# The opening of a hybrid decoder layer: zero products first, smaller first transfers, own rows and banks for the first pair, GpSimd for one product

## The chip, the core and the metric

The kernel runs on one core of one Trainium2 chip. The metric is the time of one execution in device microseconds (us). The median of three runs of the kernel before is 911.94 us (911.87 to 914.20). The data are float32; matrix products are made from high and low parts in a rounded float32 form.

## What is computed

One layer of a decoder with 512 tokens and 1024 features. Cut to what matters here:

```python
h = rmsnorm(x, g_mix)
q_sb, k_sb, v_sb, q_r, k_r, v_r, g_r, gate_sb, gate_ret = split_cols(h @ w_in)
q_sb = head_rmsnorm(to_heads(q_sb, 8), sb_q_gain)        # heads of 64
k_sb = head_rmsnorm(to_heads(k_sb, 8), sb_k_gain)
y_sb = from_heads(stick_breaking_attention(q_sb, k_sb, to_heads(v_sb, 8)))
q_r = rotary(to_heads(q_r, 8))
k_r = rotary(to_heads(k_r, 8)) * 64 ** -0.5
y_r = retention_chunkwise(q_r, k_r, to_heads(v_r, 8))
y_r = from_heads(head_rmsnorm(y_r, ret_norm_gain)) * silu(g_r)
merged = sigmoid(gate_sb) * (y_sb @ w_branch_sb) + sigmoid(gate_ret) * (y_r @ w_branch_ret)
x = x + merged @ w_out
# then a gated feed-forward block (w_up, a causal convolution, w_down) and a gated embedding
```

rmsnorm divides x by the root of its mean square over the 1024 features and multiplies by a gain per feature.

## The kernel before, in words

Features lie on partitions, so x is eight tiles of 128x512. A weight matrix is cut into chunks of 128 output columns; a chunk is eight blocks of 128x128 (512 KB) and its product with x or h is one PSUM bank. SP loads a chunk into one of three ring slots w_f, ScalarE casts it to w_hi (L644), VectorE makes w_lo = w_f - w_hi (L1068), and TensorE makes three products a block (split3, L346 to L348: high by high, high by low, low by high), 24 a chunk. The input tiles have a high and a low part in the same way.

The mixer goes by four pairs of heads. A pair takes nine chunks ("slots"), numbered 0 to 8 for the first pair: q, k, v of the attention, q and k of the retention, two of its gate, two of its v. Chunks 9 on belong to the second pair. Each engine has a program of its own, written out by hand; semaphores join them. TensorE's other work (statistics, transposes, scores, values) is hung between the blocks of chunks: a hook at place (s, k) runs behind block k of slot s (back, L495).

The first pair differs from the others, so that TensorE can begin before the norm is known. Chunks 0 to 7 are multiplied with x * g_mix (tiles T_X0), and the eviction evac_x (L1129) multiplies by A_RS = 1/rms(x), which stands in for the norm. Chunk 8 and everything later use h itself (tiles T_H), made beside chunks 2 to 8: normed (x * gain * A_RS), high_h (L812), low_h (L1125). Only chunk 8 waits for h's tiles one by one.

The opening, by engine:
- SP (L235 to L250): chunk 0, x in four transfers of two tiles, chunk 1, the constants, chunk 2, the rotary table, the decay rows; then chunks 3 to 7, each once its slot is free. Later swap_halves (L257) copies the halves of the rotary q and k.
- ScalarE: g_mix is loaded, the table loaded, w_hi of chunk 0 is cast; then x's eight tiles are cast with their gain (raw high parts), with two squares between; w_hi of chunk 1; the other six squares; w_hi of chunk 2; Ln and Exp of the mean square (A_RS).
- VectorE: w_lo of chunk 0, raw_split of the eight tiles (L1080), the sum of the squares (raw_sum, L1086), w_lo of chunks 1 and 2, six small constants, and then start() (L1286) and first_back() (L1313).
- TensorE: chunks 0, 1 and 2, with stat_x (the sum over partitions, L522) in chunk 1 and stat_qk (L366) for q's heads behind chunk 2.
- GpSimd issues seven small loads and does nothing else.

The dense banks are three (bank[s % 3]); free_bank (L476) makes slot s wait until slot s-3 is evicted. aty has three more banks: 0 for statistics and transposes, 0 and 1 for the turned weights, 2 for the values' sum. The attention of a pair is a chain over three groups of blocks: sb_scores (TensorE), sb_factors (ScalarE), sb_weights (VectorE scans), sb_turn (TensorE), sb_high and sb_low, sb_values. The values of the first head end in y_out (L749), which copies them from aty's bank 2 before the second head's values may write there. On ScalarE y_out stands behind high_rot(0, 0), the cast of the rotated q.

## Time and profile before

| | |
|---|---|
| median of three runs | 911.94 us |
| the profiled execution's own time | 913.93 us |
| its span, first to last instruction | 912.1 us |
| TensorE, work in flight | 892.4 us |
| VectorE busy | 517.4 us |
| ScalarE busy | 398.9 us |
| mean granted clock of TensorE | 0.998 of full |

The span is what the trace shows; 1.8 us of the execution lie around it. All times below are in us from the span's start. Products on TensorE overlap, so a product's length says little: their pitch, the distance between starts, is the cost. A row of the timeline gives the start, the length (of all that it merges), the engine, the line, the operation, output and inputs, the shape, how many, and, where the engine stood idle before it, for how long and what ended that.

### The profile page before, as it was taken

The page shows a single profiled execution, that of the slowest core. Times are in us where ns is not written, and L with a number is a line of the kernel's source. Part 1 is how long each engine was busy: PE and PEld are TensorE (multiplying, and loading weights), DVE is VectorE, ACT ScalarE, POOL GpSimd, SP SyncE. Part 2 cuts the span into 40 slices and gives each one's busy share as a digit, 9 for nine tenths or more (in the row PEclk, how much of TensorE's full clock was granted, in tenths as well). Part 3 has the DMA queues.
Part 4 walks back from the last instruction along what each step waited for, and adds up shares of the span by engine and source line. Part 5 has one row for each costly group of instructions (what it writes and reads, how often), then busy time and mean ns, then how long its engine had stood idle before and what let it go on. Part 6 is the DMA issues. An engine that isn't in the chain of part 4 may idle for free.

```text
span 912.1 us, 11455 instructions
## 1 busy us (share of the span) xinstructions
PE 892.4 (98%) x4070; PEld 724.4 (79%) x4070; DVE 517.4 (57%) x660; ACT 398.9 (44%) x519; POOL 4.0 (0%) x11
## 2 busy tenths in 40 slices
PE   6998999999999999999999999999999999999998
PEld 5776787787787888888887888888888888888786
DVE  6787577577677453333555666566655643333354
ACT  6636657557566442233244433333333332223431
POOL 1000000000000000000000000000000000000000
PEclk9999999999999999999999999999999999999999
DMA  7214214214213153322322332222222232322141
GB/s 275 80 36 139 81 36 138 80 35 138 80 35 127 58 196 104 104 82 91 115 94 96 115 111 92 92 92 92 100 107 92 86 104 87 103 86 93 58 143 70
DMA packets 28553, 89.93 MB, mean 99 GB/s; under 512 B 3920, under 2 KB 4960, under 8 KB 28400
## 3 DMA queue, kind: packets, MB, share of 16 engines
q1 hardware_dynamic: 27232, 85.87, 27.4%
q10 hardware_dynamic: 1072, 3.67, 1.2%
q8 instruction: 15, 0.25, 0.1%
q0 software_dynamic: 224, 0.06, 0.1%
q14 instruction: 10, 0.08, 0.0%
HBM read 84.34 MB, written 2.10 MB: 95 GB/s over the span
## 4 chain that ended last, share of the span: by engine, by line
PE 92%; DVE 4%; ACT 2%; issue 1%; DMA 1%; SPq 0%; ACTq 0%; DVEq 0%
PE dense L346 29%; PE dense L348 28%; PE dense L347 28%; PE z L402 2%; DVE fs L1068 1%; DVE w_lo L1068 1%; PE aty L431 1%; DVE fs L1071 1%; PE aty L446 1%; PE aty L391 1%; ACT fs L629 1%; ACT w_hi L644 1%; DMA fs<-in_xT 1%; PE aty L348 1%; PE aty L347 1%
## 5 line engine op out<-in xcount | busy, mean ns | idle before, releaser
L346 PE MATMUL dense<-hi,w_hi 128*128 128x512 f32 x1184 | 471.3, 398 | 9.3 <-DVE lo L1071 8.9
L348 PE MATMUL dense<-hi,w_lo 128*128 128x512 f32 x1184 | 462.7, 391 | 0.0
L347 PE MATMUL dense<-lo,w_hi 128*128 128x512 f32 x1184 | 462.6, 391 | 0.0
L1068 DVE TENSOR_TENSOR w_lo<-w_f,w_hi 128x1024 fp32r<-128x1024 f32 (+2 forms) x160 | 184.3, 1152 | 229.4 <-ACT w_hi L644 228.9
L346 PEld LDWEIGHTS dense<-hi,w_hi 128*128 128x128 f32 x1184 | 223.3, 189 | 60.4 <-issue 13.3
L348 PEld LDWEIGHTS dense<-hi,w_lo 128*128 128x128 f32 x1184 | 223.1, 188 | 47.4
L347 PEld LDWEIGHTS dense<-lo,w_hi 128*128 128x128 f32 x1184 | 223.5, 189 | 44.4 <-issue 1.2
L644 ACT CAST w_hi<-w_f 128x1024 fp32r<-128x1024 f32 (+2 forms) x160 | 158.3, 990 | 181.3 <-PE dense L348 179.0
L629 ACT ACTIVATE fs<-fs 128x512 f32<-128x512 f32 (+2 forms) x79 | 55.3, 707 | 80.7 <-DVE fs L1068 41.5
L1068 DVE TENSOR_TENSOR fs<-fs 128x512 f32<-128x512 f32 (+2 forms) x119 | 87.7, 742 | 3.9 <-ACT fs L676 0.5
L1068 DVE TENSOR_TENSOR lo<-fs,hi 128x512 fp32r<-128x512 f32 (+3 forms) x73 | 54.5, 755 | 40.9 <-ACT hi L1003 20.1
L1068 DVE TENSOR_TENSOR fs<-dense,fs 128x512 f32<-128x512 f32 x84 | 57.4, 684 | 8.4 <-ACT fs L629 5.0
L1071 DVE SCALAR_TENSOR_TENSOR fs<-fs,cw 128x512 f32<-128x512 f32 x44 | 33.1, 751 | 28.0 <-ACT fs L629 25.0
L1003 ACT CAST hi<-fs 128x512 f32 (+1 forms) x22 | 13.7, 621 | 59.5 <-DVE fs L1068 59.5
L629 ACT ACTIVATE fs<-fs,cw 128x512 f32<-128x512 f32 x22 | 17.9, 816 | 43.8 <-DVE fs L1068 43.8
L1071 DVE SCALAR_TENSOR_TENSOR lo<-fs,gain,hi 128x512 fp32r<-128x512 f32 (+1 forms) x24 | 17.7, 750 | 24.3 <-ACT hi L629 24.3
L1071 DVE SCALAR_TENSOR_TENSOR fs<-fs,gain 128x512 f32<-128x512 f32 x24 | 17.5, 748 | 20.6 <-ACT fs L629 20.6
L1244 DVE TENSOR_TENSOR_SCAN fs<-z,mrev 128x511 f32<-128x511 f32 (+3 forms) x32 | 24.1, 804 | 3.9 <-ACT z L629 3.8
L783 ACT CAST hi<-aty 128x512 fp32r<-128x512 f32 (+1 forms) x16 | 10.7, 696 | 32.4 <-PE aty L431 32.4
L727 ACT CAST hi<-z 128x1024 fp32r<-128x1024 f32 (+3 forms) x16 | 11.1, 695 | 30.9 <-DVE z L1068 30.9
L629 ACT ACTIVATE fs<-aty,eps 128x512 f32<-128x512 f32 (+1 forms) x15 | 12.0, 803 | 19.6 <-PE aty L383 8.1
L1068 DVE TENSOR_TENSOR lo<-z,hi 128x1024 fp32r<-128x1024 f32 (+3 forms) x16 | 13.2, 825 | 12.2 <-ACT hi L727 12.2
(87 smaller groups left out, 379.8 us busy)
## 6 DMA issues: line engine op xcount, KB each, us to landing
w_f<-in_w_in SPq DMA_DIRECT2D x52, 512.0 KB, 3.3
w_f<-in_w_up SPq DMA_DIRECT2D x44, 512.0 KB, 3.1
w_f<-in_w_down SPq DMA_DIRECT2D x16, 512.0 KB, 3.5
w_f<-in_w_b SPq DMA_DIRECT2D x8, 512.0 KB, 3.2
w_f<-in_w_out SPq DMA_DIRECT2D x8, 512.0 KB, 3.2
w_f<-in_w_pg SPq DMA_DIRECT2D x8, 512.0 KB, 3.2
w_f<-in_w_down SPq DMA_DIRECT2D x8, 384.0 KB, 3.0
fs<-in_xT SPq DMA_DIRECT2D x4, 512.0 KB, 7.0
```

Of the source, the lines that this page charges most:

```text
L346: mm(out, w1, x1, start=start, stop=False, skip_group_check=skip)
L347: mm(out, w1, x0, start=False, stop=False, skip_group_check=skip)
L348: return mm(out, w0, x1, start=False, stop=stop, skip_group_check=skip)
L402: ins = mm(z[:, hd, first_col:first_col + cols.stop - cols.start], wp[rows, w, i * P:(i + 1) * P], xp[rows, x, cols], start=first, stop=last)
L629: return nc.scalar.activation(out, src, func, **kw).then_inc(done, 1)
L644: nc.scalar.copy(w_hi[r][:, 0:kt, :], w_f[r][:, 0:kt, :]).then_inc(s_whi, 1)
L727: nc.scalar.copy(r_pair(hi, i), z[:, :, 0:width(i)]).then_inc(s_rahi, 1)
L783: ins = nc.scalar.copy(at_blocks(hi)[:, :, to, :], aty[:, 0:2, first:first + n].rearrange("p h (b c) -> p h b c", c=P))
L1003: nc.scalar.copy(hi[:, T_G + f, :], fs[:, A_U, :]).then_inc(s_ghi, 1)
L1068: return nc.vector.tensor_tensor(out, a, b, op).then_inc(done, 1)
L1071: return nc.vector.scalar_tensor_tensor(out=out, in0=a, scalar=scalar, in1=b, op0=op0, op1=op1).then_inc(done, 1)
L1244: nc.vector.tensor_tensor_scan(fs[:, A_CP + hd, to + skip:to + width], z[:, hd, last - skip:last - width:-1], mrev[:, skip:width], 0.0, AL ...
```

## The change

It touches only the opening and the first pair.
- Zeros: VectorE writes zeros into a tile, and TensorE makes ten products of 128x512 with it into aty's bank 2 before chunk 0.
- Loads: chunk 0 in two halves of 256 KB; x as one tile on SP, one, two and two tiles on ScalarE's queue, and two on SP. The casts and w_lo of chunk 0 are in halves too, the second ahead of x's tile 2.
- The constants made by VectorE (ones, block, mask, reversed identity) are made by GpSimd.
- stat_x moves to block 2 of chunk 2. On VectorE w_lo of chunk 2 goes ahead of the last two sums, and w_lo of chunk 3 ahead of the wait for A_RS.
- The first pair's q and k go to rows A_G and A_G+1 and no longer wait for h's first tiles, and both are evicted and squared one right behind the other.
- Slots 3 and 4 of the first pair go to aty's banks 1 and 2, so only slots 5 and 8 wait for evictions.
- x * A_RS is made by GpSimd, in place, eight products behind one another; the gain moves into high_h and low_h.
- Hooks of the first pair move: scores 1 from (5, 2) to (5, 0), scores 2 from (6, 3) to (6, 1), values and turns by one place or more.
- The order on ScalarE and VectorE in start and first_back changes with it.

```diff
-            load(0, 0, w_in[0], 8, first=True)
-            for i in range(4):
-                load_x(i)
+            sp.dma_start(w_f[0][:, 0:4, :], w_in[0][:, 0:4, :]).then_inc(s_w0, 16)
+            sp.dma_start(fs[:, A_X, :], xT[:, 0, :]).then_inc(s_x[0], 16)
+            sp.dma_start(w_f[0][:, 4:8, :], w_in[0][:, 4:8, :]).then_inc(s_wdma[0], 16)
+            sp.dma_start(fs[:, A_X + 4:A_X + 6, :], xT[:, 4:6, :]).then_inc(s_x[3], 16)
...
+            pool.wait_ge(s_xrs, 1)
+            for n in H_ORDER:
+                x = fs[:, A_X + n, :]
+                nc.gpsimd.tensor_tensor(x, x, fs[:, A_RS, :], ALU.mult).then_inc(s_hf, 1)
...
                 if g == 0:
                     pe.wait_ge(s_raw_done, RAWS * j + 3)
-                    if not isinstance(j, int):
+                    if isinstance(j, int):
+                        pe.wait_ge(s_evac, 4)
...
+            def warm_up():
+                pe.wait_ge(s_warm, 1)
+                for _ in range(10):
+                    mm(aty[:, 2, :], hi[:, T_SQ, 0:P], hi[:, T_SQ, :], start=True, stop=True)
...
-                places = {(5, 2): at(sb_scores, j, 1), (5, 3): at(sb_turn, j, 0), (6, 0): at(sb_values, j, 0, 3),
-                          (6, 3): at(sb_scores, j, 2), (6, 4): at(sb_turn, j, 1), (7, 0): at(sb_values, j, 0, 2),
-                          (7, 2): at(sb_turn, j, 2), (7, 5): at(sb_values, j, 0, 1), (7, 6): at(sb_values, j, 0, 0),
-                          (8, 0): at(sb_values, j, 1, 3), (8, 1): at(sb_values, j, 1, 2),
-                          (8, 2): at(sb_values, j, 1, 1), (8, 3): at(sb_values, j, 1, 0),
+                    places = {(3, 1): at(stat_qk, 0, 1, (s_misc, 1)), (3, 7): at(sb_scores, j, 0),
+                              (4, 2): at(turn_v, 0, 2, (s_misc, 2)), (5, 0): at(sb_scores, j, 1),
+                              (5, 2): at(sb_turn, j, 0), (5, 7): at(sb_values, j, 0, 3), (6, 1): at(sb_scores, j, 2),
+                              (6, 3): at(sb_turn, j, 1), (7, 0): at(sb_values, j, 0, 2), (7, 3): at(sb_turn, j, 2),
+                              (7, 6): at(sb_values, j, 0, 1), (7, 7): at(sb_values, j, 0, 0)}
+                    later = 1
...
+                places[8, later] = at(sb_values, j, 1, 3)
+                places[8, later + 1] = at(sb_values, j, 1, 2)
...
                 for s in range(3, SLOTS):
-                    free_bank(j, s)
+                    if prev is not None or s in (5, 8):
+                        free_bank(j, s)
...
+                    out = aty[:, s - 2, :] if prev is None and s in (3, 4) else None
...
+            warm_up()
             chunk(0, 0, 0, KD, T_X0, before={k: (s_xlo, k + 1) for k in range(KD)})
-            chunk(1, 1, 1, KD, T_X0, {6: stat_x})
-            chunk(2, 2, 2, KD, T_X0, {7: lambda: stat_qk(0, 0, (s_xrs, 1))})
+            chunk(1, 1, 1, KD, T_X0)
+            chunk(2, 2, 2, KD, T_X0, {2: stat_x, 7: lambda: stat_qk(0, 0, (s_xrs, 1))})
...
             act.dma_start(gain[:, G_MIX:G_MIX + KD, 0], g_mix).then_inc(s_gmix, 16)
+            for i, n in ((1, 1), (2, 2), (4, 6)):
+                act.dma_start(fs[:, A_X + n:A_X + n + min(i, 2), :], xT[:, n:n + min(i, 2), :]).then_inc(s_x[i], 16)
...
+            act.wait_ge(s_w0, 16)
+            nc.scalar.copy(w_hi[0][:, 0:4, :], w_f[0][:, 0:4, :]).then_inc(s_w0hi, 1)
...
+                if k == 2:
+                    act.wait_ge(s_wdma[0], 16)
+                    nc.scalar.copy(w_hi[0][:, 4:8, :], w_f[0][:, 4:8, :]).then_inc(s_whi, 1)
```

ScalarE's start() and first_back(), before and after:

```diff
                 high(0, 2, first=True)
+                ahead(0, 1)
                 act.wait_ge(s_xst, 1)
                 run(fs[:, A_RS, :], misc, ACT.Ln, s_xln, scale=1.0 / D, bias=eps[:, :])
                 act.wait_ge(s_xln, 1)
                 run(fs[:, A_RS, :], fs[:, A_RS, :], ACT.Exp, s_xrs, scale=-0.5)
+                ahead(0, 2)
+                norm_qk(0, 0, 1)
                 high_h(0)
-                ahead(0, 1)
-                high_h(1)
-                norm_qk(0, 0, 1)
-                ahead(0, 2)
                 high_qk(0, 0)
                 norm_qk(0, 1, 2)
+                high_qk(0, 1)
                 sigmoid_tables()
-                high_qk(0, 1)
-                high_h(2)
-                high_h(4)
+                high_h(1)
+                ahead(0, 3)
```

VectorE's start():

```diff
+                ahead(0, 1)
                 dve.wait_ge(s_xrs, 1)
-                normed(0)
-                normed(1)
-                low_h(0)
+                dve.wait_ge(s_cr, 2)
+                dve.wait_ge(s_cp, 6)
                 evac_x(0)
                 square(0, 0)
-                ahead(0, 1)
-                low_h(1)
                 evac_x(1)
                 square(0, 1)
-                normed(2)
+                ahead(0, 2)
                 norm(0, 0)
-                ahead(0, 2)
+                low_h(0)
                 low_qk(0, 0)
                 norm(0, 1)
                 low_qk(0, 1)
-                low_h(2)
-                normed(4)
+                low_h(1)
                 evac_x(2)
+                ahead(0, 3)
```

In VectorE's first_back() the five normed go, evac_x(6) and low_h(6) move ahead of sb_low(0, 2), and low_h(3) and low_h(5) one group later.

## Rows read from the trace of the kernel before

**Rows 1.** The page's first part: busy us, share of the span, instructions.
```profile
PE 892.4 (98%) x4070; PEld 724.4 (79%) x4070; DVE 517.4 (57%) x660; ACT 398.9 (44%) x519; POOL 4.0 (0%) x11
```

**Rows 2.** Windows: stretch, length, busy (count) by engine, clock, DMA share, GB/s.
```profile
0.00:10.00 10.00, 1.79 (x4) 1.50 (x5) 3.92 (x6) 5.64 (x8) 4.03 (x11) 1.00 0.77 266
...
70.00:80.00 10.00, 8.15 (x33) 6.92 (x34) 7.12 (x11) 8.18 (x10) 0.00 (x0) 0.83 0.59 197
```

**Rows 3.** Waits of TensorE, 0 to 140 us: total, times, longest.
```profile
PE dense L346 <- DVE lo L1071: 8.2, 1, 8.2
PE aty L446 <- ACT fs L752: 2.5, 1, 2.5
PE aty L446 <- DVE lo L1264: 1.7, 2, 1.3
PE z L402 <- DVE lo L1068: 0.6, 1, 0.6
PE aty L431 <- DVE lo L1196: 0.5, 1, 0.5
```

**Rows 4.** The chain that ended last, 0 to 8 us: start, us, what.
```profile
1.19 5.27 DMA fs<-in_xT
...
6.48 0.73 ACT hi L629
```

**Rows 5.** Timeline of TensorE, 8 to 22 us.
```profile
8.21 0.77 PE L346 MATMUL dense<-hi,w_hi 128*128 128x512 f32 x1 [8.21 <-DVE lo L1071]
...
9.20 0.63 PE L348 MATMUL dense<-hi,w_lo 128*128 128x512 f32 x1
...
13.04 0.63 PE L348 MATMUL dense<-hi,w_lo 128*128 128x512 f32 x1
...
16.41 0.39 PE L346 MATMUL dense<-hi,w_hi 128*128 128x512 f32 x1
...
21.17 1.02 PE L364 MATMUL aty<-fs,cst 128*128 128x512 f32 x2
```

**Rows 6.** Timeline of ScalarE, 0 to 24 us.
```profile
0.75 0.42 ACTq L635 DMA_DIRECT2D gain<-in_g_mix  x1
...
4.62 1.04 ACT L644 CAST w_hi<-w_f 128x1024 fp32r<-128x1024 f32 x1 [2.13 <-DMA gain<-in_g_mix]
...
13.69 3.42 ACT L629 ACTIVATE fs<-fs 128x512 f32<-128x512 f32 x6
...
22.95 0.63 ACT L629 ACTIVATE fs<-fs 128x512 f32<-128x512 f32 x1
```

**Rows 7.** Timeline of VectorE, 5 to 27 us.
```profile
5.69 1.23 DVE L1068 TENSOR_TENSOR w_lo<-w_f,w_hi 128x1024 fp32r<-128x1024 f32 x1 [4.82 <-ACT w_hi L644]
7.32 2.88 DVE L1071 SCALAR_TENSOR_TENSOR lo<-fs,gain,hi 128x512 fp32r<-128x512 f32 x4 [0.40 <-ACT hi L629]
...
14.96 4.67 DVE L1068 TENSOR_TENSOR fs<-fs 128x512 f32<-128x512 f32 x6
...
26.66 0.69 DVE L1068 TENSOR_TENSOR fs<-fs 128x512 f32<-128x512 f32 x1
```

**Rows 8.** Timeline of TensorE: behind scores 0, first of chunk 8, first of chunk 9.
```profile
37.44 0.50 PE L346 MATMUL dense<-hi,w_hi 128*128 128x512 f32 x1
...
68.51 0.39 PE L346 MATMUL dense<-hi,w_hi 128*128 128x512 f32 x1
...
80.05 0.40 PE L346 MATMUL dense<-hi,w_hi 128*128 128x512 f32 x1
```

**Rows 9.** Timeline of VectorE: the first scans, the last residue of the rotary k.
```profile
43.18 2.33 DVE L1244 TENSOR_TENSOR_SCAN fs<-z,mrev 128x511 f32<-128x511 f32 x2
...
78.67 0.69 DVE L1068 TENSOR_TENSOR lo<-fs,hi 128x512 fp32r<-128x512 f32 x1 [0.69 <-ACT hi L706]
```

**Rows 10.** Timeline of ScalarE: y_out of the first head.
```profile
71.22 0.58 ACT L752 COPY fs<-aty 128x512 f32<-128x512 f32 x1
```

**Rows 11.** Timeline of GpSimd, 0 to 10 us: one of its four memsets.
```profile
0.25 0.10 POOL L1650 MEMSET const-float32-0.0<- 128x1 f32 x1 [0.25 <-issue]
```

More of the change, by code:

```diff
@@ L119, in build @@
         s_cst, s_gmix, s_gain, s_eps, s_cr = sem("s_cst"), sem("s_gmix"), sem("s_gain"), sem("s_eps"), sem("s_cr")
-        s_x = [sem(f"s_x{i}") for i in range(4)]
+        s_x = [sem(f"s_x{i}") for i in range(5)]
+        s_warm, s_w0, s_w0hi, s_cp = sem("s_warm"), sem("s_w0"), sem("s_w0hi"), sem("s_cp")
         s_xsq, s_xst, s_rope, s_dec = sem("s_xsq"), sem("s_xst"), sem("s_rope"), sem("s_dec")
@@ L167, in a_sq, with a_raw @@
             return A_T + t if isinstance(j, int) else A_SQ
+        def a_raw(j, t):
+            return A_G + t if isinstance(j, int) else A_RAW + t
         def keys(i):
@@ L348, in split3, with chunk @@
                 return mm(out, w0, x1, start=False, stop=stop, skip_group_check=skip)
-            def chunk(c, r, b, kt, tile0, hooks=None, k_first=0, last=True, before=None):
-                pe.wait_ge(s_wlo, c + 1)
+            def chunk(c, r, b, kt, tile0, hooks=None, k_first=0, last=True, before=None, out=None):
+                if not (isinstance(c, int) and c == 0):
+                    pe.wait_ge(s_wlo, c + 1)
+                out = bank[b][:, :] if out is None else out
                 for k in range(kt):
@@ L355, in chunk @@
                         pe.wait_ge(*before[k])
-                    ins = split3(bank[b][:, :], w_hi[r][:, k, :], w_lo[r][:, k, :], hi[:, tile0 + k, :],
+                    ins = split3(out, w_hi[r][:, k, :], w_lo[r][:, k, :], hi[:, tile0 + k, :],
                                  lo[:, tile0 + k, :], start=(k_first + k == 0), stop=(last and k == kt - 1))
@@ L514, in back @@
+                places[8, later] = at(sb_values, j, 1, 3)
+                places[8, later + 1] = at(sb_values, j, 1, 2)
+                places[8, later + 2] = at(sb_values, j, 1, 1)
+                places[8, later + 3] = at(sb_values, j, 1, 0)
+                places[8, 6] = at(turn_v, j, 7, (s_atlo, 3 * j + 3))
                 for s in range(3, SLOTS):
-                    free_bank(j, s)
+                    if prev is not None or s in (5, 8):
+                        free_bank(j, s)
                     hooks = {k: places[s, k] for k in range(KD) if (s, k) in places}
@@ L519, in back @@
                               for k in range(KD)} if prev is None and s == RAW_X else None
-                    chunk(SLOTS * j + s, s % RING, s % 3, KD, T_X0 if raw else T_H, hooks, before=before)
+                    out = aty[:, s - 2, :] if prev is None and s in (3, 4) else None
+                    chunk(SLOTS * j + s, s % RING, s % 3, KD, T_X0 if raw else T_H, hooks, before=before, out=out)
             def stat_x():
@@ L840, in first_back @@
                 sb_factors(0, 0)
-                ahead(0, 3)
                 high_v(0, 0)
-                high_h(3)
+                high_h(2)
                 ahead(0, 4)
-                high_h(5)
+                high_h(4)
                 sb_high(0, 0)
                 sb_factors(0, 1)
+                high_h(3)
                 ahead(0, 5)
+                high_h(5)
                 sb_high(0, 1)
                 sb_factors(0, 2)
+                ahead(0, 6)
                 high_h(6)
-                ahead(0, 6)
                 sb_high(0, 2)
@@ L1094, in raw_sum @@
                     tt(acc, acc, sq, ALU.add, s_xacc)
-            low(0, 0)
+            dve.wait_ge(s_w0hi, 1)
+            nc.vector.tensor_tensor(w_lo[0][:, 0:4, :], w_f[0][:, 0:4, :], w_hi[0][:, 0:4, :], ALU.subtract)
             dve.wait_ge(s_gmix, 16)
             for k in range(KD):
+                if k == 2:
+                    dve.wait_ge(s_whi, 1)
+                    tt(w_lo[0][:, 4:8, :], w_f[0][:, 4:8, :], w_hi[0][:, 4:8, :], ALU.subtract, s_wlo)
                 raw_split(k)
@@ L1313, in first_back @@
             def first_back():
-                low_h(4)
-                ahead(0, 3)
-                normed(3)
                 sb_weights(0, 0)
```

95 lines of the change are left out of this document (51 added, 44 removed).

## The prediction

> **What bounds the kernel now.** I read the page's busy times first. TensorE has work in flight for 98% of the span, VectorE for 57%, ScalarE for 44%, GpSimd for almost nothing [rows 1]. So one engine sets the end, and a change gains only where it takes time from TensorE: idle time, a lower clock, or work. The windows show where that time lies: in the first 10 us TensorE works 1.79 us, and in 70 to 80 us its granted clock is 0.83 [rows 2]. The waits up to 140 us then name it: 8.2 us before the first product, and 2.5, 1.7 (in two), 0.6 and 0.5 us later [rows 3]. After the first pair hardly anything is left, so this change has the first 80 us to work in.
>
> The opening is slower than its waits. From 9.20 to 13.04 nine products start 0.427 us apart, from 16.41 to 21.17 twenty-one start 0.227 us apart [rows 5]. These are the two levels of the clock, 1.2 and 2.4 GHz, though the column of the granted clock reads 1.00 in the first 10 us [rows 2]: the pitch is the surer sign. TensorE had idled for 8.2 us before the low stretch and for 2.5 us before the second one (71.85, clock 0.83). A chunk is 24 products: 24 * 0.227 = 5.45 us at full clock. I number the chunks of w_in 0 to 8; before, chunk 0 starts at 8.21, chunk 1 at 16.41, chunk 8 at 68.51 and chunk 9 at 80.05 [rows 5, 8].
>
> **The change part by part: the start.** Before, x's first pair of tiles lands at 6.46 (1.19 + 5.27), ScalarE's cast takes 0.73 us and VectorE's residue 0.76, and TensorE starts at 8.21 [rows 4, 5]. After, 256 KB of weights and 256 KB of x replace 512 and 512 KB on SP's queue, but ScalarE's queue moves x's other tiles at the same time. ScalarE's three added issues, 0.42 us each [rows 6], delay its table load by 1.3 us, which the wait to 4.62 covers. The first tile is bounded below by g_mix, which released ScalarE at 4.62 [rows 6], and above by today's 6.46. I take 5.0: cast to 5.7, residue to 6.5, TensorE at 6.6, 1.6 us earlier (bounds 0 to 2.0).
>
> From there VectorE paces chunk 0, not TensorE. It does eight residues at 0.72 us (2.88 for four), two sums (0.4 and 0.6), and now also the second half of w_lo, 0.6 us (half of 1.23) [rows 7]. That half waits for the second weight transfer and its cast; I put it at 7.4 to 8.1. Six residues and two sums later it is 13.3; w_lo of chunk 1 ends at 14.7. TensorE, at 0.68 us a tile, follows and starts chunk 1 at 14.8, where it was 16.41: 1.6 us. The full clock gains nothing beyond that, and TensorE could stay at the low level until near 11 us without being later. So the ten zero products (10 * 0.427 = 4.3 us, from 1.5 on, before any real work can start) cost nothing and are worth between 0 and 1.5 us.
>
> **Sum of x squared.** stat_x moves from chunk 1, tile 6, to chunk 2, tile 2. VectorE sums four squares (0.76 each), makes w_lo of chunk 2 (1.22, after ScalarE's cast that follows six squares of 0.57), sums two more and ends near 20.6 [rows 6, 7]. Chunk 2 starts at 20.3, stat_x is at 22.3, so TensorE doesn't wait. From stat_x to the end of Exp it is 2.4 us (21.17 to 22.95 + 0.63 [rows 5, 6]); 1/rms is there at 24.7, against 23.6. The six small constants move to GpSimd beside this; as they stood they took VectorE 1.4 us that nobody waited for.
>
> **q and k.** Before, VectorE does two products of x, two residues and two w_lo among the q and k steps; now q and k have rows A_G and A_G+1, and chunks 3 and 4 go to aty's banks 1 and 2, so TensorE needs no eviction before chunk 5. I walk it with single durations (0.69 for 512 columns and 1.22 for w_lo [rows 7], 0.63 for Exp and about the same for Ln [rows 6], and the 2.4 us again from a statistic to its Exp): eviction 25.4, square 26.1, stat_qk 26.6, Exp 29.0, norm 29.8, second Ln 30.4 to 31.7, norm 32.5, cast 33.1, residue 33.8. TensorE ends chunk 3 at 33.9, and its first scores no longer wait: their 0.6 us [rows 3] goes. Chunk 4 begins at 35.0, against 37.44 [rows 8]: 2.4 us ahead in all.
>
> **The middle.** The new places put scores 1 at (5,0), 2 at (6,1), and the values one or more tiles later. Two scans take 2.33 us [rows 9], so the first are done at 40.5, before (5,0) at 41.6; the turn at 44.1 finds v's residue (43.0) and the weights (41.7). values(0,3) comes at 48.5 against 47.4. Scores 2 come at 50.3, the scans end at 50.8: a new stall of 0.5. The next turn and values find their data. So the two stalls before today's values (1.7 together [rows 3]) and 0.5 of the first turn go, 0.5 comes, and shorter switches give 0.4: 2.1 us. Chunk 8 begins 4.5 us ahead, near 64.0.
>
> **Chunk 8** takes 11.5 us today. values(1,3) wait 2.5 us for ScalarE's copy y_out (71.22 [rows 10]), queued behind the cast of the rotated q, which waits for VectorE; then the clock is low: 0.83 over 10 us [rows 2] is 3.4 us at half speed, which costs 1.7. After, VectorE ends the first q's rotation at 64.2 (behind it no product of x any more), y_out ends at 65.4, and TensorE, now two tiles into the chunk, is at 65.3. The wait of 2.5 shrinks to 0.1 or so, the clock stays: with 0.2 for a switch, 3.9 us gained. Ahead by 8.4 us, chunk 9 starts near 71.6.
>
> **What is late next.** The second rotation doesn't move as much: VectorE still waits for chunk 7 and for the swap that SP starts after s_rot. low_rot(0,1), today at 78.67 to 79.36 [rows 9] with over 2 us in hand, would end at 73.0; r_scores ask at 73.0; then turn_v waits 0.45 for low_v(0,1), and r_scores 1 0.1. I book 0.8 back (bounds 0 to 2.5). SP's loads behind the swaps still land before their casts. Ahead: 7.6 us.
>
> **GpSimd.** It now makes eight products x * 1/rms of 128x512 from 24.7 on. No row shows such an operation on it: the nearest are a memset of one column, 0.10 us [rows 11], and VectorE's product of the same size, 0.69 [rows 7]. Alone it is hidden: the first is wanted by 29.0 (4.3 us), the second by 34.4 (9.7 us for two), later ones later still. ScalarE waits for them, and behind that high_h(1) stand w_hi of chunk 5 and the factors of the scores. But GpSimd works beside VectorE for the first time, in the stretch where VectorE's chain leads. There VectorE has ten operations, 7.6 us, in 9.1 us, so 1.5 us of slack, and eight of them read two tensors from SBUF. If each waits w, the delay is 8w - 1.5. With w = 0 it is nothing, with w a whole product of 0.69 it is 4.0 us. I take half a product, 1.3 us. (The Trainium skill, "SBUF — State Buffer", section "Who interferes with whom", says that a VectorE instruction with two SBUF inputs contends with a GpSimd instruction that reads SBUF. "GPSIMD Engine Reference", section "3. Performance versus the Vector engine", gives GpSimd 1.96 times VectorE's time for such an operation, by which a product would be 1.35 us, an estimate, and with whole products waited for the delay 9.3 us. No run here shows either yet.)
>
> **Sum.** 1.6 (start) + 0 (pace, same 1.6 at chunk 1) + 0.8 (scores) + 2.1 + 3.9 = 8.4; less 0.8 and 1.3: 6.3 us. Profiled, 913.93 - 6.3 = 907.6 with a span of 905.8. That execution is 2.0 above the median of 911.94, and the forecast stands against the median: 905.6 us.
>
> **Rivals.**
> 1. The wait that replaces the removed ones: VectorE and GpSimd hold each other up by whole products, w from 0.69 to 1.35. Then the scores come 4.0 to 9.3 us late and the gain is 3.6 to -1.7: 908.3 to 913.6, middle 911. For it: the eight operations lie just in that stretch; against: VectorE has gaps of its own there, waiting for Ln and Exp. Chance 0.20. (The skill's rule in its strict form is this case.)
> 2. The transfers aren't sooner. Weights and x share the same total rate over two queues; x's first tile lands at 6.46 as today. VectorE's pace from there gives chunk 1 at 16.1, 1.3 us later than booked: 906.9, to 908 if the clock is low too. Chance 0.15.
> 3. It ends slower: the same mutual wait with w over 1.15 us takes all of the 7.6, and over 1.5 us makes the kernel more than 0.3% slower. At w = 1.7 the delay is 12.1 us: 916.4. It would need a GpSimd product over twice VectorE's. Chance 0.07.
> 4. No contention and nothing given back: 911.94 - 8.4 = 903.5, and to 902 if other steps come out better. Chance 0.08.
>
> My forecast, with a delay between 0 and 3 us, has the remaining 0.50. Over 0.3% (2.7 us, about what a measurement of this kernel can tell from no change) means below 909.2 or above 914.7. Faster: 0.50 + 0.15 + 0.08 and a fifth of rival 1, 0.77; within: 0.16; slower: 0.07. The range from 902.0 to 910.0 takes in all but the worse half of rival 1 and rival 3.
>
> **What would show it.** Right: first real product at 6.2 to 7.4; ten products before it at 0.43 us; chunk 1 at 14.8; no wait before the first scores; values(1,3) waiting under 0.7 us with the pitch at 0.227; chunk 9 near 73. Wrong: VectorE's squares, norms and residues between 24 and 36 us longer than 0.69, or starting late with their inputs ready; GpSimd products over 1.4 us; ScalarE waiting for GpSimd before high_h(1); or waits of TensorE over 1 us in the first chunks of pair 1.

## The result, and the profile after

The changed kernel takes 915.61 us, median of eleven runs (914.60 to 915.96). The kernel before, run beside it, takes 913.72 (eleven runs, 911.67 to 914.97). The ratio is 1.0025, with a 95% interval of 1.0015 to 1.0035. That is 0.25% slower, inside the 0.3% that the prediction called no change, and 10 us above its 905.6. The three runs shown before the prediction had a median of 911.94; 1.8 us of the 10 are that. The times of the kernel before fall into two groups, which the mean granted clock tells apart: of 29 later executions twelve read 1.00 and took 911.45 to 912.23 us, seventeen read 0.996 or 0.998 and took 913.21 to 915.31. The median of 911.94 lies in the first group, the profiled execution (913.93, clock 0.998, low in chunk 8 [rows 2]) in the second. None of the changed kernel's eleven runs reads 1.00 (0.992 to 0.998).

The profiled execution took 915.40 us with a span of 913.6. Comparing starts on TensorE in the traces splits the difference of the spans. The column e1 is the first experiment below (GpSimd's products cut to one column each); "forecast" is the prediction's own walk.

| us | before | after | e1 | forecast |
|---|---|---|---|---|
| start of chunk 1 | 16.41 | 16.90 | 17.21 | 14.8 |
| chunk 1 to scores 0 | 20.14 | 24.34 | 19.30 | 20.6 |
| scores 0 to chunk 8 | 31.96 | 32.06 | 29.53 | 29.9 |
| chunk 8 | 11.54 | 7.74 | 7.74 | 7.6 |
| chunk 9 to the end | 832.05 | 832.56 | 832.52 | 832.9 |
| span | 912.1 | 913.6 | 906.3 | 905.8 |

Three things stand in it: the opening isn't faster, chunk 8 gives what it should (3.8 of 3.9), and the stretch before the first scores has grown by 4.2 us.

The page's first part, to set beside [rows 1]: TensorE's work is what it was plus ten products, and GpSimd now has work.

```profile
PE 895.8 (98%) x4080; PEld 725.8 (79%) x4080; DVE 518.8 (57%) x649; ACT 400.2 (44%) x520; POOL 22.2 (2%) x25
```

VectorE has 11 instructions less and is busy 1.4 us more. Eight products of about 0.7 us (5.6 us), some small constants and more have left it, so what stayed must have become longer. That is visible before any timeline is opened.

The waits of TensorE from 0 to 140 us, where [rows 3] stood before (total, times, longest):

```profile
PE z L419 <- DVE lo L1109: 5.1, 2, 4.9
PE dense L361 <- DVE lo L1112: 3.8, 4, 1.5
PE aty L501 <- DVE hi L1121: 1.5, 1, 1.5
...
PE aty L467 <- ACT fs L792: 0.2, 1, 0.2
```

The 8.2 us wait at the start has been cut into 1.5 before the zeros and 3.8 before and in chunk 0, the wait for y_out has gone from 2.5 to 0.2, and the 1.7 before the first values is gone. On top stands a new one: 4.9 us before the first scores, for a residue of VectorE. It was 0.6.

The windows (stretch, length, busy and count of TensorE, its weight loads, VectorE, ScalarE and GpSimd, then clock, DMA share, GB/s), as in [rows 2]:

```profile
30.00:40.00 10.00, 6.38 (x27) 4.58 (x25) 9.51 (x6) 4.23 (x7) 10.00 (x6) 1.00 0.14 54
...
40.00:50.00 10.00, 8.76 (x31) 6.57 (x32) 8.34 (x11) 7.57 (x11) 0.63 (x1) 0.66 0.15 52
```

From 30 to 40 us VectorE is busy 9.51 us with six instructions, 1.6 us each, while GpSimd has no gap. From 40 to 50 the clock is at 0.66.

TensorE's timeline gives the starts of the table and the price of the low clock, against [rows 5, 8]:

```profile
1.49 4.57 PE L501 MATMUL aty<-hi 128*128 128x512 f32 x10 [1.49 <-DVE hi L1121]
...
7.44 0.50 PE L361 MATMUL dense<-hi,w_hi 128*128 128x512 f32 x1 [1.37 <-DVE lo L1112]
...
16.90 0.50 PE L361 MATMUL dense<-hi,w_hi 128*128 128x512 f32 x1 [0.44 <-DVE w_lo L1109]
...
41.24 0.80 PE L419 MATMUL z<-hi 64*128 64x512 f32 x2 [4.86 <-DVE lo L1109]
...
43.41 0.63 PE L362 MATMUL aty<-lo,w_hi 128*128 128x512 f32 x1
...
45.97 0.63 PE L362 MATMUL aty<-lo,w_hi 128*128 128x512 f32 x1
...
73.30 0.39 PE L361 MATMUL dense<-hi,w_hi 128*128 128x512 f32 x1
```

From 43.41 to 45.97 lie six products, 0.427 us each: after idling for 4.86 us TensorE is at 1.2 GHz, half of its full speed, until 46.8 us. In the kernel before it idled 0.6 us here and stayed at the full level.

### The profile page after: what moved, and what is told of

It is laid out like the page before. It is cut to its first block, busy times and chain, and to the rows that moved or that the text cites. A ratio compares the mean times of both kernels' runs of the same rounds, so it can differ in the third digit from the quotient of the medians.

```text
span 913.6 us, 11479 instructions
## 1 busy us (share of the span) xinstructions
PE 895.8 (98%) x4080; PEld 725.8 (79%) x4080; DVE 518.8 (57%) x649; ACT 400.2 (44%) x520; POOL 22.2 (2%) x25
## 4 chain that ended last, share of the span: by engine, by line
PE 92%; DVE 4%; ACT 2%; DMA 1%; issue 0%; SPq 0%; ACTq 0%; DVEq 0%
PE dense L361 28%; PE dense L363 28%; PE dense L362 28%; PE z L419 2%; DVE fs L1109 1%; DMA fs<-in_xT 1%; PE aty L450 1%; DVE w_lo L1109 1%; PE aty L361 1%; PE aty L363 1%; PE aty L362 1%; DVE lo L1112 1%; PE aty L408 1%; PE aty L467 0%; DVE fs L1112 0%
## 5 line engine op out<-in xcount | busy, mean ns | idle before, releaser
L361 PE MATMUL dense<-hi,w_hi 128*128 128x512 f32 x1168 | 462.8, 396 | 5.3 <-DVE lo L1112 4.5
L363 PE MATMUL dense<-hi,w_lo 128*128 128x512 f32 x1168 | 455.1, 390 | 0.0
L362 PE MATMUL dense<-lo,w_hi 128*128 128x512 f32 x1168 | 455.0, 390 | 0.0
L361 PEld LDWEIGHTS dense<-hi,w_hi 128*128 128x128 f32 x1168 | 219.3, 188 | 57.3 <-DVE lo L1112 7.4
L363 PEld LDWEIGHTS dense<-hi,w_lo 128*128 128x128 f32 x1168 | 219.2, 188 | 46.4
L362 PEld LDWEIGHTS dense<-lo,w_hi 128*128 128x128 f32 x1168 | 219.5, 188 | 43.1 <-issue 0.7
L1109 DVE TENSOR_TENSOR lo<-fs,hi 128x512 f32 (+3 forms) x65 | 50.5, 785 | 40.2 <-ACT hi L1044 20.1
L1112 DVE SCALAR_TENSOR_TENSOR lo<-fs,gain,hi 128x512 fp32r<-128x512 f32 (+1 forms) x32 | 24.7, 783 | 26.8 <-ACT hi L664 25.8
L1112 DVE SCALAR_TENSOR_TENSOR fs<-fs,gain 128x512 f32<-128x512 f32 x16 | 13.7, 877 | 18.9 <-ACT fs L664 18.9
L1308 DVE TENSOR_TENSOR lo<-aty,hi 128x512 fp32r<-128x512 f32 (+1 forms) x16 | 12.8, 822 | 14.6 <-ACT hi L823 14.6
```

The lines of the kernel that those rows point to most:

```text
L361: mm(out, w1, x1, start=start, stop=False, skip_group_check=skip)
L362: mm(out, w1, x0, start=False, stop=False, skip_group_check=skip)
L363: return mm(out, w0, x1, start=False, stop=stop, skip_group_check=skip)
L1109: return nc.vector.tensor_tensor(out, a, b, op).then_inc(done, 1)
L1112: return nc.vector.scalar_tensor_tensor(out=out, in0=a, scalar=scalar, in1=b, op0=op0, op1=op1).then_inc(done, 1)
L1308: ins = nc.vector.tensor_tensor(at_blocks(lo)[:, :, to, :], aty[:, 0:2, first:first + n].rearrange("p h (b c) -> p h b c", c=P), at_blocks ...
```

## The cause on VectorE

GpSimd's eight products are one row of its timeline, and VectorE's work beside them ten:

```profile
27.01 13.62 POOL L352 TENSOR_TENSOR fs<-fs 128x512 f32<-128x512 f32 x8 [8.98 <-ACT fs L664]
```

```profile
26.96 0.69 DVE L1109 TENSOR_TENSOR fs<-dense,fs 128x512 f32<-128x512 f32 x1 [2.78 <-ACT fs L664]
27.69 1.17 DVE L1109 TENSOR_TENSOR fs<-fs 128x512 f32<-128x512 f32 x1
28.78 0.68 DVE L1109 TENSOR_TENSOR fs<-dense,fs 128x512 f32<-128x512 f32 x1
29.49 1.04 DVE L1109 TENSOR_TENSOR fs<-fs 128x512 f32<-128x512 f32 x1
30.46 2.31 DVE L1109 TENSOR_TENSOR w_lo<-w_f,w_hi 128x1024 fp32r<-128x1024 f32 x1
32.70 1.78 DVE L1112 SCALAR_TENSOR_TENSOR fs<-fs,gain 128x512 f32<-128x512 f32 x1
34.40 1.77 DVE L1112 SCALAR_TENSOR_TENSOR lo<-fs,gain,hi 128x512 fp32r<-128x512 f32 x1
36.10 1.75 DVE L1109 TENSOR_TENSOR lo<-fs,hi 128x512 fp32r<-128x512 f32 x1
37.77 1.75 DVE L1112 SCALAR_TENSOR_TENSOR fs<-fs,gain 128x512 f32<-128x512 f32 x1
40.20 0.99 DVE L1109 TENSOR_TENSOR lo<-fs,hi 128x512 fp32r<-128x512 f32 x1 [0.69 <-ACT hi L742]
```

The two evictions (fs<-dense,fs) read one tensor from PSUM and one from SBUF: 0.69 and 0.68, as before [rows 7]. All the others read twice from SBUF: 0.99 to 1.78 in place of about 0.7, 2.31 in place of 1.22. The least stretched are the two squares, which read one tensor twice (1.17 and 1.04), and the last, beside which GpSimd ends. Nothing starts late; the operations themselves are longer. These are the eight that the prediction named. From 32.70 on the two engines go in step: VectorE starts an operation at 32.70, 34.40, 36.10 and 37.77, and GpSimd makes its eight in 13.62 us, 1.70 each. Whether one stands still while the other reads, or both read at a lower rate, these rows can't tell.

## The experiments

Each is the changed kernel with one edit, unless said otherwise. The kernel before ran beside every group; the medians of those runs lie between 913.4 and 913.8, and each ratio is taken against them.

**e1: take GpSimd's products away, keep their order and waits.** Only one column of each x tile is multiplied by 1/rms.

```diff
-                nc.gpsimd.tensor_tensor(x, x, fs[:, A_RS, :], ALU.mult).then_inc(s_hf, 1)
+                nc.gpsimd.tensor_tensor(x[:, 0:1], x[:, 0:1], fs[:, A_RS, 0:1], ALU.mult).then_inc(s_hf, 1)
```

> The changed kernel with GpSimd's eight products of x made on one column instead of 512 (the rest of h isn't scaled: work left out). Theory, contention: VectorE's squares, norms and residues between 27 and 41 us take 0.69 to 0.75 us again instead of 1.0 to 1.8, low_qk(0,1) ends near 35.5, the scores' wait falls from 4.9 to under 0.5 us, the clock doesn't fall, so 4.7 + 2.3 = 7 us less: about 908.7 us. Rival, order: the operations put ahead of the norms (w_lo of chunk 4, low_h(0)) make the scores late; then the wait stays above 3 us and the time near 914. Rival, late 1/rms: the same, because stat_x came at 24.5.

Measured: 908.21 us, ratio 0.9950 (0.9935 to 0.9965). VectorE's same operations, from its timeline:

```profile
28.04 0.72 DVE L1109 TENSOR_TENSOR fs<-fs 128x512 f32<-128x512 f32 x1
...
30.00 1.22 DVE L1109 TENSOR_TENSOR w_lo<-w_f,w_hi 128x1024 fp32r<-128x1024 f32 x1
31.62 0.76 DVE L1112 SCALAR_TENSOR_TENSOR fs<-fs,gain 128x512 f32<-128x512 f32 x1 [0.40 <-ACT fs L664]
...
33.06 0.69 DVE L1109 TENSOR_TENSOR lo<-fs,hi 128x512 fp32r<-128x512 f32 x1
```

The stretch is gone, operation by operation; over the eight it had been 6.3 us (0.45 + 0.35 + 1.09 + 1.02 + 1.02 + 1.06 + 0.99 + 0.30). The scores start at 36.51 in place of 41.24. The price of the products is 915.61 - 908.21 = 7.4 us: 4.7 of later scores (5.0 counted from chunk 1), and 2.5 in the stretch behind them (32.06 against 29.53), where the clock now reads 1.00 in 40 to 50 us. These 2.5 lie where the clock was low: from the first scores to the next transposes it is 5.59 us in the change (41.24 to 46.83) and 3.06 here (36.51 to 39.57), for the same products.

**e6: the products back on VectorE, in its gaps.** Eight instructions normed(k), where the changed order waits for ScalarE anyway.

```diff
-            for n in H_ORDER:
-                x = fs[:, A_X + n, :]
-                nc.gpsimd.tensor_tensor(x, x, fs[:, A_RS, :], ALU.mult).then_inc(s_hf, 1)
...
+                normed(0)
                 norm(0, 0)
                 low_h(0)
                 low_qk(0, 0)
+                normed(1)
                 norm(0, 1)
+                normed(2)
                 low_qk(0, 1)
+                normed(4)
+                normed(3)
                 low_h(1)
```

> The changed kernel with x times 1/rms back on VectorE (eight products of 0.69 us, put in VectorE's gaps), nothing else undone. Theory: VectorE has 4.8 us more to do but none of its operations is stretched, so the scores wait under 1 us and the time is within 1.5 us above the 908.2 of the kernel with one-column products: 908.5 to 909.7, faster than both. Rival, VectorE's load: the eight products cost 0.6 us each on the chain and the time is 912 to 913.

Measured: 909.02 us, ratio 0.9952 (0.9936 to 0.9968); scores at 37.11. (One of its six executions took 3563.4 us, and one of the kernel before beside it 2303.9; neither is in the ratio, and without it the median is 908.89.) With all the work done, it costs 0.8 us more than e1, with none of it done (within the runs' scatter), and 6.6 us less than GpSimd doing it. VectorE has gaps for its eight products of about 0.65 us; as GpSimd's neighbour it loses 6.3 us.

**e8: is it any work of GpSimd, or two tensors read at once?** The product becomes one by a constant 1.0, with one tensor read (1/rms is left out).

```diff
-                nc.gpsimd.tensor_tensor(x, x, fs[:, A_RS, :], ALU.mult).then_inc(s_hf, 1)
+                nc.gpsimd.tensor_scalar(x, x, 1.0, None, ALU.mult).then_inc(s_hf, 1)
```

> The changed kernel with GpSimd's eight products by a tensor replaced by products by the constant 1.0 (one input instead of two; x isn't scaled: work left out). If what holds VectorE up is each access of GpSimd to SBUF, VectorE's two-input operations between 27 and 41 us are still stretched, but by about half (1.0 to 1.3 us), and the scores wait 1.5 to 3 us: 911 to 913. If only a second input of GpSimd's collides, they take 0.7 us and the time is near 908.5.

Measured: 908.88 us, ratio 0.9952 (0.9934 to 0.9970). GpSimd is as busy as ever, and VectorE hardly notices:

```profile
27.48 12.97 POOL L352 TENSOR_SCALAR fs<-fs 128x512 f32<-128x512 f32 x8 [9.32 <-ACT fs L664]
```

```profile
30.09 1.22 DVE L1109 TENSOR_TENSOR w_lo<-w_f,w_hi 128x1024 fp32r<-128x1024 f32 x1
...
33.17 0.99 DVE L1109 TENSOR_TENSOR lo<-fs,hi 128x512 fp32r<-128x512 f32 x1
34.43 1.19 DVE L1112 SCALAR_TENSOR_TENSOR fs<-fs,gain 128x512 f32<-128x512 f32 x1 [0.26 <-ACT fs L664]
```

GpSimd's eight, by their source line (shortest, median and longest in ns):

```profile
L352 POOL TENSOR_SCALAR fs<-fs x8: 1482/1496/2249, 27.5 to 38.8; 128x512 f32<-128x512 f32 x8
```

w_lo keeps its 1.22 us, and the worst operation is 1.19 in place of 0.76. The eight lose 0.8 us together (0.30, 0.43 and 0.08 on three of them) where they had lost 6.3. So with one tensor read GpSimd still collides with VectorE, but little of it falls on VectorE: it is GpSimd's product beside w_lo that takes 2.25 us, where its median is 1.50. Nearly all of the price hangs on GpSimd's second tensor, or on the kind of operation, which changed with it; no run separates these two. e8 also clears GpSimd's slowness as such: its results come nearly as late as with the real products (the last at 40.45 against 40.63), and nothing waits for them long enough to matter.

**e11: the kernel before, with only the products moved to GpSimd.** High_h and low_h take the gain, as in the change; nothing else is touched.

```diff
+            pool.wait_ge(s_xrs, 1)
+            for n in H_ORDER:
+                x = fs[:, A_X + n, :]
+                nc.gpsimd.tensor_tensor(x, x, fs[:, A_RS, :], ALU.mult).then_inc(s_hf, 1)
...
-                nc.scalar.copy(hi[:, T_H + k, :], fs[:, A_X + k, :]).then_inc(s_hhi, 1)
+                nc.scalar.activation(hi[:, T_H + k, :], fs[:, A_X + k, :], ACT.Identity,
+                                     scale=gain[:, G_MIX + k, :]).then_inc(s_hhi, 1)
```

> The kernel before with one part of the change alone: x times 1/rms on GpSimd, the gain in the high and low parts of h. Theory, contention: VectorE's two-input operations from 24 to 38 us are stretched from 0.69 to 1.0 to 1.8 us, which costs more than the four products of 0.75 us that leave VectorE there; the scores come 3 to 6 us later than 36.55, the clock falls in the wait, and the time is 4 to 8 us longer than the kernel before: 917 to 922 us. Rival, it was the new order that made it costly: the time is within 2 us of before.

Measured: 912.76 us, ratio 0.9993 (0.9983 to 1.0003): a miss for me. The stretch is there (w_lo at 2.28 us) and the scores are 4.6 us late (41.16 against 36.55), as expected, but the end is not. Its waits behind the start's show why (1.5 is that for y_out, 2.5 before):

```profile
PE aty L368 <- DVE fs L1073: 1.8, 2, 1.6
PE aty L450 <- ACT fs L756: 1.5, 1, 1.5
PE z L406 <- DVE lo L1073: 1.3, 1, 1.3
PE dense L350 <- DVE w_lo L1073: 1.2, 1, 1.2
```

```profile
28.90 2.28 DVE L1073 TENSOR_TENSOR w_lo<-w_f,w_hi 128x1024 fp32r<-128x1024 f32 x1
```

The delay is taken in pieces of 1.2 to 1.6 us, since chunks wait for evictions between, and no window from 30 to 80 us has a clock under 1.00. Behind the scores it gets back 3.0 us up to chunk 8 (28.97 against 31.96) and 2.5 in chunk 8 (9.03 against 11.54), where VectorE and the clock were what TensorE waited for before. The changed kernel has hardly any such waits left: with everything else of the change in place, moving the products only lost. The same edit makes next to no difference in one order of work and costs 6.6 us in the other (915.61 against e6's 909.02). Next to none, since e11's twelve runs all read a clock of 1.00 or 0.999: it is 1.0 us slower than the runs of the kernel before that read 1.00 (median 911.73 in this group), and 1.4 faster than the median of the others, 914.14. That the removed waits decide is read from these two traces; no run puts them back into the changed kernel.

**e3: the first transfers and casts of the kernel before, in the changed kernel.**

```diff
+            load(0, 0, w_in[0], 8, first=True)
+            for i in range(4):
+                sp.dma_start(fs[:, A_X + 2 * i:A_X + 2 * i + 2, :], xT[:, 2 * i:2 * i + 2, :]).then_inc(s_x[i], 16)
...
-            for i, n in ((1, 1), (2, 2), (4, 6)):
-                act.dma_start(fs[:, A_X + n:A_X + n + min(i, 2), :], xT[:, n:n + min(i, 2), :]).then_inc(s_x[i], 16)
```

> The changed kernel with the first transfers, casts and the residue of chunk 0 as before the change; zero products, order and GpSimd stay. Theory: TensorE starts at 8.2 with the full clock, VectorE's pace ends chunk 1's w_lo at 15.1, chunk 1 starts near 15.2 against 16.9, so 1.7 us less: 913.9 us; the new transfers alone would then cost 1.7 us. Rival: the new transfers do help (first product 0.8 us sooner) and this kernel is 0.8 us slower, 916.4.

Measured: 914.03 us (914.45 profiled), ratio 1.0007 (0.9997 to 1.0017): 1.6 us faster than the change. The first product starts later, at 8.63 against 7.44, and chunk 1 sooner, at 16.09 against 16.90. The two kernels' runs don't overlap (913.08 to 914.58 against 914.60 to 915.96). So the early start of TensorE bought nothing.

**e2: the small transfers, all on SP's queue in the order of need.**

```diff
             sp.dma_start(fs[:, A_X, :], xT[:, 0, :]).then_inc(s_x[0], 16)
+            sp.dma_start(fs[:, A_X + 1, :], xT[:, 1, :]).then_inc(s_x[1], 16)
             sp.dma_start(w_f[0][:, 4:8, :], w_in[0][:, 4:8, :]).then_inc(s_wdma[0], 16)
-            sp.dma_start(fs[:, A_X + 4:A_X + 6, :], xT[:, 4:6, :]).then_inc(s_x[3], 16)
+            for i in (2, 3, 4):
+                n = 2 * i - 2
+                sp.dma_start(fs[:, A_X + n:A_X + n + 2, :], xT[:, n:n + 2, :]).then_inc(s_x[i], 16)
```

> The changed kernel with all first transfers on SP's queue in the order in which they are used: half of chunk 0, x tile 0, tile 1, other half, then x's pairs. Theory, order of arrival: the second half of chunk 0's weights lands near 6.5 instead of 8.4, chunk 1 starts near 15.0 instead of 16.9, and stat_x, the scores and the end come 1.8 us earlier: 913.8 us. Rival, total rate: the two queues share one rate and the same bytes must land either way, so chunk 1 starts within 0.4 us of 16.9.

Measured: 914.96 us, ratio 1.0021 (1.0011 to 1.0032), chunk 1 at 16.74, where 15.0 was expected; it stayed within the rival's 0.4 us of 16.90. The order over the two queues is worth some 0.65 us, less than what the opening lacks, and the interval overlaps the change's.

**e5: GpSimd's seven small loads after x.**

```diff
+            pool.wait_ge(s_x[4], 16)
             for col, src, n in
```

> The changed kernel with GpSimd's seven small loads (gains and convolution weights, 0.06 MB) issued only once x's last pair has landed. Theory, small packets: from 3 to 6 us the DMA engines are 0.83 to 1.03 busy but move only 156 to 253 GB/s, because the small packets of the gains take turns with the weights' and x's; without them the second half of chunk 0's weights lands near 7 instead of 8.4, chunk 1 starts near 15.4 instead of 16.9, and the time is 1.5 us less than the changed kernel's 915.6: 914.1. Rival, smaller transfers are slow by themselves: the landings stay within 0.4 us and the time too.

Measured: 914.72 us, ratio 1.0016 (1.0005 to 1.0027), chunk 1 at 16.53; 0.9 us faster than the change, with overlapping intervals, and not all of it is the loads'. In the profiled executions, 1.3 us apart, chunk 1 comes 0.4 sooner; 1.0 lies behind the scores, where after the same wait (4.85 us) the clock of 40 to 50 us reads 0.83 in place of 0.66. The windows of 3 to 6 us, first of the change, then of this kernel:

```profile
3.00:4.00 1.00, 1.00 (x4) 0.81 (x3) 0.00 (x0) 0.99 (x2) 1.00 (x3) 1.00 1.03 253
4.00:5.00 1.00, 1.00 (x3) 0.78 (x3) 0.43 (x1) 0.54 (x1) 1.00 (x3) 1.00 0.83 205
5.00:6.00 1.00, 1.00 (x3) 0.33 (x1) 0.27 (x1) 0.20 (x1) 0.65 (x2) 1.00 0.94 156
```

```profile
3.00:4.00 1.00, 1.00 (x4) 0.81 (x3) 0.00 (x0) 0.99 (x2) 0.00 (x0) 1.00 0.88 199
4.00:5.00 1.00, 1.00 (x3) 0.78 (x3) 0.41 (x1) 0.56 (x1) 0.00 (x0) 1.00 0.93 266
5.00:6.00 1.00, 1.00 (x3) 0.33 (x1) 0.28 (x1) 0.44 (x1) 0.00 (x0) 1.00 0.95 336
```

The last number is GB/s, the one before it the busy share of the DMA engines. With the small loads in flight the engines are as busy in these 3 us (2.80 against 2.76) and move 614 KB in place of 801. Over all traces with the change's new transfers or e2's it is 544 to 614 KB with the loads early (the change, e1, e2, e4, e6, e8) and 711 to 801 with them late (e5, e7, e10): the sign holds, the size varies. With the old transfers it doesn't show: 721 to 901 early (the kernel before, e3, e11), 806 and 818 late (e12, e9).

**e7: e6 and e5 together.**

> Both: x times 1/rms on VectorE, and GpSimd's small loads after x's last pair. If the two gains add, the time is 1.5 us below the one with the products on VectorE alone, near 907.5; if chunk 1's start doesn't move, they are the same.

Measured: 907.95 us, ratio 0.9945 (0.9929 to 0.9960); chunk 1 at 16.18, scores at 35.55. The late loads are worth 1.1 us here, with the clock at 1.00 behind the scores in both; e6's chunk 1 came at 17.73.

**e9: e7 with the first transfers of the kernel before.**

> The changed kernel with x times 1/rms on VectorE, GpSimd's small loads late, and the first transfers as before the change (512 KB each, all on SP). If larger transfers move x and the weights sooner, as they seemed to with the small loads early (1.6 us), chunk 1 starts near 15.2 and the time is about 907.0, 1 us under the one with the new transfers (907.95). If the small loads were all that slowed the new transfers, both kernels are within 0.5 us of each other.

Measured: 906.72 us, ratio 0.9929 (0.9914 to 0.9944); chunk 1 at 15.12, scores at 34.52, chunk 9 at 72.07. The best of all, 0.7% under the kernel before. The interval overlaps that of e7, so that the old transfers are better than the small ones rests on e3, and on the table's chunk 1.

**e4: without the ten zero products**, and **e10: e7 without them**.

```diff
-            warm_up()
```

> The changed kernel without the ten zero products. Theory, VectorE's pace: chunk 0 waits for VectorE's residues, so TensorE at the low level in it costs little: the pitch is 0.43 until 10 to 14 us, chunk 1 starts at 16.9 to 17.5, and the time is 0 to 0.6 us longer. Rival, the clock counts: chunk 0 takes 24 * 0.43 = 10.3 us from 7.4, chunk 1 starts at 17.8 or later and stays low for a part, 1 to 3 us longer.

> The changed kernel with x times 1/rms on VectorE and GpSimd's small loads late, without the ten zero products. If chunk 0 is paced by VectorE whatever the clock, the time stays within 0.5 us of 907.95. If the earlier data now leaves TensorE's low clock as the limit of chunk 0, chunk 1 starts 1 us or more later and the time is near 909.

Measured: e4 915.51 us, ratio 1.0025 (1.0015 to 1.0035), 0.1 from the change; e10 908.32, ratio 0.9942 (0.9928 to 0.9957), 0.4 from e7. In e4 the clock is low for six products and full from 11.20:

```profile
9.91 0.63 PE L363 MATMUL dense<-hi,w_lo 128*128 128x512 f32 x1
11.20 0.50 PE L361 MATMUL dense<-hi,w_hi 128*128 128x512 f32 x1 [0.67 <-DVE lo L1111]
```

Here TensorE waits for VectorE's residues in chunk 0 at either level (the bracket), so the level hardly matters. In e10, where the data comes sooner, it does:

```profile
11.69 0.63 PE L359 MATMUL dense<-lo,w_hi 128*128 128x512 f32 x1
...
15.53 0.62 PE L359 MATMUL dense<-lo,w_hi 128*128 128x512 f32 x1
```

```profile
15.32 1.22 DVE L1105 TENSOR_TENSOR w_lo<-w_f,w_hi 128x1024 fp32r<-128x1024 f32 x1
```

From 11.69 to 15.53 products start 0.427 us apart without a wait. VectorE has chunk 1's w_lo ready at 16.54, and TensorE, still in chunk 0, starts chunk 1 only at 17.62, against 16.18 in e7. That is the 1 us or more of the expectation's second case, in one execution (908.84, the longest of its six). In the medians the zeros are worth 0.1 and 0.4 us, within the runs' scatter. Nor do they always do what they are for: in the change's trace no product of chunk 0 is at half speed, in e5's and e7's, with the same zeros, the first six are.

**e12: e9 with two products (tiles 5 and 6) on GpSimd beside VectorE's first scans.** VectorE's normed(5) and normed(6) go.

```diff
+            pool.wait_ge(s_hf, 5)
+            pool.wait_ge(s_f, 1)
+            for n in (5, 6):
+                x = fs[:, A_X + n, :]
+                nc.gpsimd.tensor_tensor(x, x, fs[:, A_RS, :], ALU.mult).then_inc(s_hf, 1)
```

> The kernel with x times 1/rms on VectorE, late small loads and the old first transfers (906.72 us), with two of the eight products (tiles 5 and 6) on GpSimd, started when VectorE starts the first scans, which read one tensor from SBUF and one from PSUM. Theory, only VectorE's operations with two SBUF inputs are held up: the two scans still take 2.33 us together, the product behind them (1.22) is stretched to 1.5 to 2.5, and since VectorE gives up 1.3 us of products later, the waits for the second scans and y_out (0.6 each) shrink: 905.8 to 906.7. Rival, any VectorE operation is held up: the scans take over 3 us, and the time is 907.5 or more.

Measured: 907.72 us, ratio 0.9937 (0.9923 to 0.9951).

```profile
40.29 2.55 POOL L354 TENSOR_TENSOR fs<-fs 128x512 f32<-128x512 f32 x2 [21.72 <-ACT z L665]
```

```profile
40.25 2.33 DVE L1284 TENSOR_TENSOR_SCAN fs<-z,mrev 128x511 f32<-128x511 f32 x2 [0.28 <-ACT z L665]
42.61 1.31 DVE L1105 TENSOR_TENSOR fs<-fs 128x1024 f32<-128x1024 f32 x1
```

The scans take 2.33 us, as alone [rows 9], and GpSimd's product 1.28 (2.55 for two) in place of 1.70. The product behind the scans takes 1.31 in place of 1.22, not the 1.5 to 2.5 expected: GpSimd was all but done. So there are neighbours beside which GpSimd's work is free. The total, expected at 905.8 to 906.7, shows no gain. In its profiled execution chunk 1 came 1.6 us later than in e9, and its trace tells why:

```profile
9.18 0.63 PE L363 MATMUL dense<-lo,w_hi 128*128 128x512 f32 x1
...
13.44 0.63 PE L364 MATMUL dense<-hi,w_lo 128*128 128x512 f32 x1
```

```profile
14.03 1.22 DVE L1105 TENSOR_TENSOR w_lo<-w_f,w_hi 128x1024 fp32r<-128x1024 f32 x1
```

The first twelve products of chunk 0 are at half speed in spite of the zeros. TensorE doesn't wait once in the chunk, VectorE has chunk 1's w_lo ready at 15.25 (15.06 in e9), and chunk 1 starts at 16.74; in e9 all of chunk 0 is at full speed and chunk 1 starts at 15.12. The edit acts only later: with these transfers the level of TensorE's clock sets the start of chunk 1, and behind the same zeros it was full in one execution and not in the other. So it was in the kernel before, without zeros: w_lo of chunk 1 ready at 15.03, twelve products at half speed, chunk 1 at 16.41. From the scores to chunk 9 e12 took 37.3 us against 37.6. Whether two offloaded products pay is left open.

## Why the prediction was wrong, point by point

**Start, 1.6 us forecast, -0.5 measured: wrong.** Three terms of the walk were too small. The first product came at 7.44, not 6.6. The second half of chunk 0's weights, which I put at 7.4 to 8.1 with its w_lo, was cast only from 8.44, and x's tiles 4 and 5 from 11.28, both behind a DMA:

```profile
5.80 1.33 ACT L664 ACTIVATE hi<-fs,gain 128x512 fp32r<-128x512 f32 x2 [1.26 <-DMA fs<-in_xT]
...
8.44 0.62 ACT L695 CAST w_hi<-w_f 128x512 fp32r<-128x512 f32 x1 [1.31 <-DMA w_f<-in_w_in]
...
11.28 1.33 ACT L664 ACTIVATE hi<-fs,gain 128x512 fp32r<-128x512 f32 x2 [0.43 <-DMA fs<-in_xT]
```

I costed the order of the transfers and not their rate. This was my rival 2, with its mechanism nearly right (same total rate) and its size too kind. The small loads on GpSimd's queue, which both kernels have, account for 0.4 to 1.1 us (e5, e7), the two queues perhaps for 0.6 (e2). Why the smaller transfers end a little later than the larger ones (e3) stays open; single landings vary by about 1 us from one execution to the next. That VectorE and not TensorE paces chunk 0 was right for the changed kernel (e4), and wrong where the data comes sooner: there the level of the clock sets chunk 1 back by 1.1 us (e10) and 1.5 us (e12).

**Chain of q and k, 0.8 us forecast: right but for GpSimd.** Without contention, from chunk 1 to the scores it is 19.30 us (e1) against 20.14 before, 0.84 gained.

**Middle, 2.1 us: right but for the clock.** e1 gains 2.4. In the changed kernel it is all taken by half speed after the long wait (2.5 us, see e1); the forecast had no such term.

**Chunk 8, 3.9 us: right.** 3.8, by the mechanism named: the wait for y_out is 0.2, and the clock is full. **Given back, 0.8: right,** 0.5.

**GpSimd, 1.3 us forecast, 7.4 measured: the step that failed.** The mechanism, the place and the eight operations were right. w, the time lost by each, was taken as 0.35 and measured as 6.3 / 8 = 0.79 on the mean (0.30 to 1.09). The formula then gives 8 * 0.79 - 1.5 = 4.8, and the scores came 4.7 us later, 5.0 counted from chunk 1. Half a product was a choice between two ends with no row behind it. The nearest measured figure, a whole product of VectorE, would have given 4.0. The Trainium skill names this collision in "SBUF — State Buffer", section "Who interferes with whom", and gives GpSimd's price in "GPSIMD Engine Reference", section "3. Performance versus the Vector engine", as a ratio from which I had estimated 1.35 us: 1.28 was measured beside scans. The rule holds in its direction (evictions from PSUM untouched, two-input operations hit), and for e8's operation with one tensor too, which reads SBUF as well. The sizes are this case's: 0.99 to 1.78 us for VectorE's operations of 128x512 beside the first, up to 1.19 beside the second.

The rest, 2.5 us, is a step that wasn't in the sum at all. The delay fell on one wait of 4.9 us, and the clock was low behind it; that it fell on one because banks and rows of their own had removed the small ones before it is argued from e11, not shown. Rival 1 at w = 0.8 gives 904.3 without contention plus 4.9, 909.2; add 2.1 for the opening, 2.5 for the clock and 1.8 for the median of before, and it is 915.6, the time measured. That it meets to the tenth is luck: the middle and what was given back came out 0.3 us better each, and are not in it.

**The reference, 1.8 of the 10 us.** The forecast took its gains from the profiled execution, 1.7 us of them from a clock that is low in chunk 8, and then went down 2.0 us to a median among the times whose clock reads 1.00. A mean of 1.00 leaves no room for such a stretch, so most likely the same 1.7 us were counted twice; no trace of such an execution was kept. By its own gains the forecast was 907.3 (911.94 less 4.6) to 907.6.

**Chances.** The case I gave 0.50 fell; rival 1 and rival 2 both came true, which I had not priced together. The slow side would have needed w over 1.15 by my sum; with the opening lost and the clock low, 0.8 was enough.

## What to carry to other kernels

Before work is given to GpSimd, list what VectorE does in the same microseconds: beside operations with two tensors in SBUF a two-tensor product on GpSimd cost VectorE more (6.3 us for eight) than doing the products itself (some 5.2 us), while scans and evictions from PSUM took no longer beside it. Where the small waits ahead of a chain are gone, its delay can fall on one wait, and a long one also costs clock: price a delay as its length plus the slow stretch behind it. Judge an earlier start by when the engine that paces the stage is done, not by when TensorE begins. And look at the single times and their clock before a median of three is taken for the kernel's time.
